# Opening of a two-block transformer kernel: 14 of the first adaLN's 32 weight blocks become one-column products on TensorE

## What is computed

```python
c_act = jax.nn.silu(c)
for l in range(DEPTH):                                    # DEPTH = 2
    mod = c_act @ w_ada[l] + b_ada[l]
    sh1, sc1, gt1, sh2, sc2, gt2 = [m[:, None, :] for m in jnp.split(mod, 6, axis=-1)]
    h = rms_norm(x, norm_mix[l]) * (1.0 + sc1) + sh1
    proj = h @ w_in[l]
    ...
x = x + ...
```

## Time and profile before

| | before |
|---|---|
| median of 3 runs | 2664.87 us |
| lowest, highest | 2664.43, 2666.22 us |
| the profiled execution's own time | 2667.91 us |
| its span | 2666.1 us |
| PE busy | 2528.7 us (95%) |
| DVE busy | 1451.2 us (54%) |
| ACT busy | 1084.1 us (41%) |
| POOL busy | 1043.4 us (39%) |
| HBM read | 267.85 MB |

### The profile page before, as it was taken

One profiled execution on the slowest core, in us unless ns is written; L12 is line 12 of the kernel. 1 busy time (PEld: TensorE's weight loads), 2 busy tenths in 40 slices (PEclk: granted clock), 3 DMA queues, 4 the chain that ended last, 5 costly groups with the idle time before them and its releaser, 6 DMA issues. The chain is left out here.

```text
span 2666.1 us, 33330 instructions
## 1 busy us (share of the span) xinstructions
PE 2528.7 (95%) x13145; PEld 2039.1 (76%) x13145; DVE 1451.2 (54%) x2429; ACT 1084.1 (41%) x1904; POOL 1043.4 (39%) x560
## 2 busy tenths in 40 slices
PE   5999999999989999999999999999999998999998
PEld 3777777887868888867777878787888886776787
DVE  6399658654555545646994652363444207836322
ACT  3446663245333332234665523533333223336532
POOL 1556622112434444335664221244444444322342
PEclk8999998999989999999999999999999999999999
DMA  7221426634324426532232252322322335731232
GB/s 245 79 73 55 143 78 173 185 111 146 126 79 142 142 95 215 199 110 72 64 127 80 58 136 81 119 85 77 107 95 95 95 102 140 156 96 40 72 127 78
DMA packets 331391, 299.94 MB, mean 113 GB/s; under 512 B 56718, under 2 KB 302820, under 8 KB 330212
## 3 DMA queue, kind: packets, MB, share of 16 engines
q1 hardware_dynamic: 279268, 279.46, 33.5%
q10 hardware_dynamic: 51968, 18.35, 2.7%
HBM read 267.85 MB, written 29.93 MB: 112 GB/s over the span
## 5 line engine op out<-in xcount | busy, mean ns | idle before, releaser
L217 POOL TENSOR_TENSOR split<-ring,split 128x1024 fp32r<-128x1024 f32 (+2 forms) x340 | 806.8, 2374 | 1234.2 <-ACT split L213 1193.7
L277 PE MATMUL ps<-hh,split 128*128 128x512 f32 x3808 | 1244.7, 401 | 12.3 <-ACT wk L1987 7.1
L277 PEld LDWEIGHTS ps<-hh,split 128*128 128x128 f32 x3808 | 717.7, 189 | 175.2 <-issue 27.9
L277 PE MATMUL ps<-hl,split 128*128 128x512 f32 x1904 | 758.5, 398 | 0.0
L213 ACT ACTIVATE split<-ring 128x1024 fp32r<-128x1024 f32 (+1 forms) x336 | 341.3, 1017 | 855.4 <-PE ps L277 648.2
L277 PEld LDWEIGHTS ps<-hl,split 128*128 128x128 f32 x1904 | 364.1, 191 | 76.1 <-issue 8.4
L277 PE MATMUL ps<-split 128*128 128x512 f32 x1152 | 280.8, 401 | 0.1
L277 PEld LDWEIGHTS ps<-split 128*128 128x128 f32 x1152 | 216.0, 188 | 59.5 <-issue 14.4
L612 POOL TENSOR_TENSOR split<-ring,split 128x1024 fp32r<-128x1024 f32 x32 | 76.5, 2390 | 313.2 <-ACT split L604 313.2
L2281 PE MATMUL ps<-split 128*128 128x512 f32 x704 | 174.4, 401 | 0.0
L2281 PEld LDWEIGHTS ps<-split 128*128 128x128 f32 x704 | 136.3, 195 | 28.8
(11 more groups left out here) (422 smaller groups left out, 3383.4 us busy)
## 6 DMA issues: line engine op xcount, KB each, us to landing
ring<-in_w_in_dram SPq DMA_DIRECT2D x60, 1024.0 KB, 5.2
ring<-in_w_up_dram SPq DMA_DIRECT2D x44, 1024.0 KB, 5.1
ring<-in_w_in_dram SPq DMA_DIRECT2D x34, 512.0 KB, 5.0
big<-in_w_ada_dram SPq DMA_DIRECT2D x16, 1024.0 KB, 8.9
ring<-in_w_ada_dram SPq DMA_DIRECT2D x32, 512.0 KB, 3.6
spare<-in_w_ada_dram SPq DMA_DIRECT2D x16, 1024.0 KB, 7.5
ring<-in_w_down_dram SPq DMA_DIRECT2D x16, 896.0 KB, 5.3
ring<-in_w_swa_out_dram SPq DMA_DIRECT2D x8, 1024.0 KB, 5.2
```

Source lines behind the costliest of these rows:

```text
L217: on.tensor_tensor(halves(pt, nk)[1], slot(n, nk)[:, :, e * P:(e + 1) * P], halves(pt, nk)[0], ALU.subtract).then_inc(low_made, 1)
L277: ins = nc.tensor.matmul(ps[bank[gt]][:, :], w[:, k, :], rhs[e][:, k, :], start=(n == 0), stop=(n == 3 * nk - 1))
```

## The change

- **TensorE takes over 14 blocks.** OPENING_ADDED = (0, 8, 4, 6) says how many of a group's eight blocks VectorE still adds up: none of group 0, all of group 1, four of group 2, six of group 3. For every other block TensorE makes four fp32 products of a 128x128 piece of the weights (stationary) with one column, silu(c) of that block, adding up in PSUM (opening_close). Where VectorE added some, the product with the ones comes last.
- **TensorE's order** is: transpose of c, close 0 (32 products), the transposes of x, turn_rows, the eight mix_totals, then close 1 (4 products), close 2 (16 + 4) and close 3 (8 + 4).
- **VectorE's order** is: silu, angles, the sign of the sines, the sum of group 1, keep_rows, the sum of group 2, the sum of group 3, first_mod.
- **Eight homes** instead of four (the other four in the array spare), each with its own semaphore.
- **SyncE's order** is: c, identity, constants, positions, halves 0 and 1, x, halves 2 to 7, TM, SW. The 19 small loads of load_rows go to ScalarE's queue, behind its first activation.

```diff
+            OPENING_ADDED = (0, KD, 4, 6)
...
+                if h % homes >= 4:
+                    return spare[:, 4 * (h % 4):4 * (h % 4) + 4, :]
...
+            def opening_sum(dve, m):
+
+                acc, n = first_sum[:, m % 2, :], OPENING_ADDED[m]
+                for k in range(n):
+                    h = 2 * m + k // 4
+                    if k % 4 == 0:
+                        dve.wait_ge(first_in[h], 16)
+                    w = first_half(h, N_ADA)[:, k % 4, :]
+                    if k == 0:
+                        if m >= 2:
+                            dve.wait_ge(first_made, m - 1)
+                        nc.vector.tensor_scalar(acc, w, c_act[:, 0:1], None, ALU.mult).then_inc(first_added, 1)
+                    else:
+                        dve.wait_ge(first_added, sum(OPENING_ADDED[:m]) + k)
+                        nc.vector.scalar_tensor_tensor(out=acc, in0=w, scalar=c_act[:, k:k + 1], in1=acc, op0=ALU.mult,
+                                                       op1=ALU.add).then_inc(first_added, 1)
+
+            def opening_close(pe, m):
+
+                n = OPENING_ADDED[m]
+                if n:
+                    pe.wait_ge(first_added, sum(OPENING_ADDED[:m + 1]))
+                for h in (2 * m, 2 * m + 1):
+                    if n < 4 * (h - 2 * m) + 4:
+                        pe.wait_ge(first_in[h], 16)
+                for e in range(4):
+                    column = ps[5][:, 4 * m + e:4 * m + e + 1]
+                    for k in range(n, KD):
+                        w = first_half(2 * m + k // 4, N_ADA)[:, k % 4, e * P:(e + 1) * P]
+                        ins = nc.tensor.matmul(column, w, c_act[:, k:k + 1], start=(k == n), stop=(n == 0 and k == KD - 1))
+                    if n:
+                        ins = nc.tensor.matmul(column, first_sum[:, m % 2, e * P:(e + 1) * P], ones[:, 0:1],
+                                               start=(n == KD), stop=True)
+                ins.then_inc(first_made, 1)
...
@@ sync @@
+                        sp.dma_start(cst[:, P:n_const], d["consts"][:, P:n_const]).then_inc(cst_in, 16)
                         sp.dma_start(posi, d["positions"][0, :].partition_broadcast(P)).then_inc(pos_in, 16)
-                        sp.dma_start(cst[:, P:n_const], d["consts"][:, P:n_const]).then_inc(cst_in, 16)
-                        for h in range(4):
-                            load_first(sp, 0, h, 4)
+                        for h in range(2):
+                            load_first(sp, 0, h, N_ADA)
                         for t in range(TT):
                             sp.dma_start(xt[:, t, :], d["x"][0, t * P:(t + 1) * P, :]).then_inc(x_in[t], 16)
-                        load_rows(sp, 0)
+                        for h in range(2, N_ADA):
+                            load_first(sp, 0, h, N_ADA)
                         load_early(sp, 0, TM)
-                        for h in range(4, N_ADA):
-                            load_first(sp, 0, h, 4)
                         load_early(sp, 0, SW)
@@ tensor @@
                         pe.wait_ge(cst_in, 16)
-                        close_first(pe, 0)
+                        pe.wait_ge(c_step, 3)
+                        opening_close(pe, 0)
...
-                        close_first(pe, 1)
                         turn_rows(pe)
                         for k in range(KD):
                             mix_total(pe, k)
-                        close_first(pe, 2)
-                        close_first(pe, 3)
+                        for m in range(1, N_ADA // 2):
+                            opening_close(pe, m)
@@ scalar @@
+                        load_rows(act, 0)
@@ vector @@
-                        for h in range(N_ADA):
-                            if h == 2:
-                                dve.wait_ge(sin_step, 1)
-                                nc.vector.tensor_scalar(sin_t[:, :], sin_t[:, :], const("turn_sign"), None, ALU.mult)
-                            if h == 6:
-                                keep_rows(dve)
-                            add_first(dve, h, 4)
+                        dve.wait_ge(sin_step, 1)
+                        nc.vector.tensor_scalar(sin_t[:, :], sin_t[:, :], const("turn_sign"), None, ALU.mult)
+                        opening_sum(dve, 1)
+                        keep_rows(dve)
+                        opening_sum(dve, 2)
+                        opening_sum(dve, 3)
                         first_mod(dve)
```

More of the change, by code:

```diff
@@ L342, in clear_all @@
                 nc.multi_engine_barrier(list(nc.engines), sems_to_clear=range(min(layer_sems), max(layer_sems) + 1))
-            first_in = [sem(f"first_in{e}") for e in range(4)]
+            first_in = [sem(f"first_in{e}") for e in range(N_ADA)]
             first_added, first_made = sem("first_added"), sem("first_made")
```

## The result

The changed kernel took 2670.08 us (median of 13 runs, 2662.64 to 2672.16) against 2662.37 us for the kernel before (13 runs beside it, 2659.78 to 2666.98). The ratio is 1.0020, 95% interval 1.0012 to 1.0029: +5.3 us (+3.2 to +7.7). The two medians lie 7.7 us apart and the two means 5.4 us; the ratio with its interval is what is compared from here on. The forecast was +8.3. In a second measurement the ratio was 1.0008 (0.9997 to 1.0018), +2.1 us (-0.8 to +4.8). So the change costs a few microseconds, clearly so in the first measurement only, and less than forecast: +8.3 lies just above the first interval and well above the second. Single runs of one kernel spread over 7 to 14 us, which is why the traces are read for places and the repeated runs for times.

The account below looks back on a forecast made before the run. Bound: half 4's late landing, then 16 VectorE blocks, four narrow products, the gain. Half 1 14.7, close 0 28.5, squares 44.1, VectorE 51.4, close 3 56.7, gain 57.2 against 48.9: +8.3, 2673.2 us; range 2666.5 to 2676.5.

Parts of the forecast that it names:

- Half 1 and the small loads: Opening's loads: small loads on ScalarE's queue delay half 1 by 0 to 2.2 us, 1.0 taken, landing at 14.7 us.
- The price of a narrow product: Group 0 on TensorE: 64 instructions at the slow 0.214 us spacing, 13.8 us, close 0 ending at 28.5 us.
- the step on which everything rested: TensorE's opening: one-column products neither raise nor hold the clock, so 0.214 us each for group 0, not 0.10.
- From x to the squares: First transpose of x to last product over the squares: again 15.57 us, squares summed at 44.1 us.
- my bound of 1.6: Stretch from x to the squares: clock rising earlier or later in the transposes makes -1.5 to +1.6 us.
- The late products: Behind the squares: close 1 to 45.0, VectorE's group 3 to 51.4, close 3 5.3 us to 56.7, gain 57.2 us.
- GpSimd's collision: VectorE's sum of group 3: GpSimd's TM subtraction holds up one instruction, costing 2.0 us more.
- nothing behind the barrier makes up for it: Behind the opening: TensorE idles through the barrier and starts the layer at 0.50 as before, so 8.3 us later remains.
- My rivals: Three cases for TensorE's clock in the opening: -1 to -4 us, +5.5 us and +1.7 us; chance 0.10 each.
- Rival 2: Opening: group 0 at the slow price, late products at the fast one; +5.5 us, 2670.4 us; chance 0.10.

Follow-up runs that it names:

- before_apart: Kernel before plus one wait: GpSimd's last subtraction ahead of the feed-forward norm waits for VectorE's last sum, in both layers; ratio 0.9983 to before.
- after_apart: Changed kernel plus one wait: GpSimd's last subtraction ahead of the feed-forward norm waits for VectorE's last sum; ratio 1.0014 to before.
- early_narrow: Changed kernel's loads, but TensorE makes only group 0's blocks, as narrow products; VectorE adds up groups 1 to 3; ratio 0.9981 to before.
- close1_early: Changed kernel with close 1 back in its old place, behind the transposes of x instead of behind the squares; ratio 1.0006 to before.
- early_wide: As early_narrow, with group 0's operands exchanged: silu(c) column stationary, 512 columns of the block moving; ratio 0.9976 to before.
- late_narrow: Changed kernel's loads, but TensorE makes only the six late blocks of groups 2 and 3, as narrow products; ratio 0.9983 to before.
- before_late: Kernel before with twelve unused VectorE instructions ahead of first_mod, so that its opening ends later; ratio 1.0007 to before.
- late_wide: As late_narrow, with the six late blocks made as products with the block as moving operand (512 columns); ratio 0.9986 to before.

## Why the prediction was right or wrong

**Half 1 and the small loads.** The first narrow product began at 13.85 us; I took 14.7 and bounded 13.7 to 15.9. The small loads cost half 1 nothing that can be seen. From 5 to 7 us the DMA rate was 180 GB/s against 298 in before, but from 4 to 5 us it was 319 against 166. Within the bound, and oversized by 0.9 us.

**The price of a narrow product.** This was right: 64 instructions from 13.85 to 27.63, 13.78 us against 13.8. The choice between 0.214 and 0.10 us was the step on which everything rested, and rows 7 and 8 had it.

**From x to the squares.** I took 15.57 us from one trace. The changed kernel needed 17.9, 18.4 and 18.4, and two more traces of before 18.5 and 18.0. The first trace of before was the one in which the clock did not fall between the transposes and the squares. The term was too small by 2.3 to 2.9 us, and my bound of 1.6 too narrow. The transposes raised the clock here too (0.213, then 0.11 us), after 5.1 us at the slow spacing. The Trainium skill's rule (TensorE: Matmul & The Clock Gate, Part 4: PE-mode transpose) stays contradicted by this.

**The late products.** VectorE's wait for TensorE (9.07 us), GpSimd's collision and the last closing are there. The collision hit the first instruction of the sum, 1.58 us instead of 0.48, so it cost 1.1 us and not 2.0. Close 3 took 5.28 us from 51.93 (5.3 forecast). The clock fell at 49.7 us, I had said about 47. End of the gain: 57.70 us against 57.2. That this agrees is partly luck: half 1 was 0.9 us too late, the squares' term 2.3 too short, the collision 0.9 too dear, and they nearly cancel. The other end of the difference was taken from one trace, and it was the latest of three: the gain of before ends at 47.87 us on average, so the openings are 10 us apart and not 8.3. Counted to the first product it is 9.7.

**What failed** is the sentence "nothing behind the barrier makes up for it". It looked at the first 10 us of the layer and took 2614 us behind it as fixed. They were 6.4 us less in the changed kernel on average, and 4.5 us (1.6 to 7.5) of that is one collision of VectorE and GpSimd in layer 0, which comes with VectorE's instruction list as it is in before and is gone from the changed one. Against the forecast's +8.3 stand +5.3 and +2.1; that before_apart and after_apart are 8.3 us apart fits to the digit by chance. My rivals were all about the clock within the opening. None was about the order of two other engines 700 us later, and the range of +1.6 to +11.6 holds both results only because it had been opened for other reasons. Rival 2's 2670.4 us is nearly the first result (2664.87 x 1.0020 = 2670.2), but its mechanism isn't what happened: it had the last closing at 2.55 us, and it took 5.28.

**What stays open.** What the 0.35 us pause of VectorE at 753 us is, and why its place moves with the list. The same seven traces have a second such difference: from the gain to VectorE's first instruction of the layer it is 1.45 to 1.51 us in them and 1.05 to 1.11 in all others. A list of VectorE that is shifted by an instruction or two with the opening left alone would have tested the first; that wasn't run. The 1 us up to 490 us and 2 us within the feed-forward part have not been assigned either.

## What to carry to other kernels

Idle TensorE time is not cheap time for matrix times vector. With the matrix as the stationary operand a product has one moving column and costs a full weight load (the 64 loads of group 0 took 13.73 of its 13.78 us), and here it neither raised the clock nor kept it up longer than an idle engine did; with the vector stationary and 512 columns moving, TensorE reached full clock and kept it. In an engine that works in program order, put such a product where nothing on the critical chain stands behind it, and check what shares its buffer. When an edit changes how many instructions an engine has, or moves a whole stage, look for places further on where two engines start within 0.2 us of one another and one blocks the other: they can give back or take away as much as the edit. Take the baseline from several traces, since one opening of before differed from the next by 1.8 us.

## What the runs showed of the hardware

- Fp32 products with one moving column, back to back for 13.8 us, never raised TensorE's clock (changed kernel, early_narrow, close1_early); in early_wide it rose 5.9 us after the first product of 512 columns, and 3 to 6 us into 128-column transposes in all traces that had it low there.
- Behind wide work the clock fell 2.2 us (late_narrow) to 5.2 us (close1_early) after the last square product with narrow products running, and 4.3 to 4.6 us after it in before's traces with TensorE mostly idle; between executions of one kernel it also falls or doesn't ahead of the squares (before: no, yes, yes).
- A VectorE sum of two SBUF operands that starts 0.19 us behind a GpSimd subtraction takes 2.70 us instead of 0.69. The Trainium skill (SBUF — State Buffer, Practical consequences) states this exclusion; the trace agrees. A one-input instruction was held up as well, 1.58 us instead of 0.48 (L413 at 46.29 us).
- VectorE paused 0.35 us more than usual at one place of its instruction list, the same place in seven traces at times 8 us apart, and at another with twelve instructions more ahead (before_late).
- In late_wide, alternating stationary operands of one row and of 128 rows cost 0.155 us an instruction at full clock, against 0.10 for the plain closings.
